# Pre-norm sums from the fourth job's third step to the fifth job's first step, their spread to the third, in a two-block transformer kernel

## What is computed

```python
def rmsnorm(x, g):
    xf = x.astype(jnp.float32)
    y = xf * lax.rsqrt(jnp.mean(xf * xf, axis=-1, keepdims=True) + EPS)
    return (y * g.astype(jnp.float32)).astype(x.dtype)

def swiglu(x, w_gu, w_down):
    gate, up = jnp.split(x @ w_gu, 2, axis=-1)
    return (jax.nn.silu(gate) * up) @ w_down
...
        y = swiglu(rmsnorm(h, ffn1_pre_g[l]), ffn1_w_gu[l], ffn1_w_down[l])
        h = h + 0.5 * rmsnorm(y, ffn1_post_g[l])
        u = rmsnorm(h, mix_pre_g[l])
        proj = u @ w_in[l]
```

## Time and profile before

| | us |
|---|---|
| median of 3 runs (3285.89 to 3286.72) | 3286.0 |
| the profiled execution | 3285.14 |
| its span, first to last instruction | 3283.3 |
| PE busy, of the span | 3253.5 (99%) |
| DVE busy | 2376.6 (72%) |
| ACT busy | 1696.0 (52%) |
| POOL busy | 319.4 (10%) |
| granted TensorE clock, mean | 0.999 |

### The profile page before, as it was taken

The page is one execution under the profiler, slowest core; times in us unless marked ns, Lnnn a source line. Parts: engine busy times, 40 slices in busy tenths (PEclk is TensorE's granted clock), DMA queues, the critical chain, the costliest instruction groups (busy, mean ns, idle before and its releaser), DMA issues.

```text
span 3283.3 us, 51624 instructions
## 1 busy us (share of the span) xinstructions
PE 3253.5 (99%) x20356; PEld 2902.7 (88%) x20356; DVE 2376.6 (72%) x4254; ACT 1696.0 (52%) x3071; POOL 319.4 (10%) x289
## 2 busy tenths in 40 slices
PE   9999999999999999999999999999999999999998
PEld 7999888888899998999888888899988888889998
DVE  7877765766687768776765776697868676658776
ACT  5555553645465545554553654464547374336553
POOL 1000110121010001000200121010000001201000
PEclk9999999999999999999999999999999999999999
DMA  4333433253233332333424253233322222322332
GB/s 142 109 104 123 120 86 87 81 155 91 81 100 105 108 103 89 105 109 110 123 76 119 59 151 103 68 106 105 115 96 92 88 82 69 105 96 96 102 112 84
DMA packets 118562, 332.80 MB, mean 101 GB/s; under 512 B 18984, under 2 KB 21800, under 8 KB 118320
## 3 DMA queue, kind: packets, MB, share of 16 engines
q1 hardware_dynamic: 106352, 308.40, 30.0%
q0 software_dynamic: 11680, 20.56, 3.1%
q10 hardware_dynamic: 288, 0.52, 0.0%
HBM read 306.23 MB, written 4.21 MB: 95 GB/s over the span
## 4 chain that ended last, share of the span: by engine, by line
PE 90%; DVE 7%; ACT 1%; issue 1%; DMA 0%; POOL 0%; DVEq 0%; ACTq 0%
PE PS L827 89%; PE PS L1231 2%; DVE h L2017 1%; DVE acc L1962 1%; DVE tmp L2014 1%; DVE ul L1970 1%; DVE wl L1933 1%; ACT wh L1350 0%; DMA tmp<-tmp 0%; ACT uh L1350 0%; ACT tmp L1350 0%; ACT stk L1350 0%; DVE y_u L2042 0%; DVE lru L2761 0%; DVE stk L2428 0%
## 5 line engine op out<-in xcount | busy, mean ns | idle before, releaser
L1933 DVE TENSOR_TENSOR wl<-raw,wh 128x1024 fp32r<-128x1024 f32 (+2 forms) x633 | 654.3, 1037 | 253.8 <-ACT wh L1350 248.1
L1350 ACT ACTIVATE wh<-raw 128x1024 fp32r<-128x1024 f32 (+2 forms) x637 | 554.1, 875 | 355.2 <-PE PS L827 342.4
L827 PE MATMUL PS<-bh,wh 128*128 128x256 f32 x2520 | 696.3, 276 | 0.0
L827 PE MATMUL PS<-bh,wl 128*128 128x256 f32 x2520 | 696.3, 276 | 0.0
L827 PE MATMUL PS<-bl,wh 128*128 128x256 f32 x2520 | 695.9, 276 | 0.0
L827 PE MATMUL PS<-uh,wh 128*128 128x512 f32 (+2 forms) x1656 | 613.8, 371 | 9.4 <-DVE ul L1970 4.0
L827 PE MATMUL PS<-ul,wh 128*128 128x512 f32 (+2 forms) x1656 | 598.6, 361 | 0.0
L827 PE MATMUL PS<-uh,wl 128*128 128x512 f32 (+2 forms) x1656 | 598.4, 361 | 0.0
L827 PEld LDWEIGHTS PS<-bh,wh 128*128 128x128 f32 x2520 | 473.1, 188 | 0.6
L827 PEld LDWEIGHTS PS<-bh,wl 128*128 128x128 f32 x2520 | 473.0, 188 | 0.6
L827 PEld LDWEIGHTS PS<-bl,wh 128*128 128x128 f32 x2520 | 473.1, 188 | 0.0
(11 more groups left out here) (272 smaller groups left out, 5366.8 us busy)
## 6 DMA issues: line engine op xcount, KB each, us to landing
raw<-in_gu SPq DMA_DIRECT2D x218, 512.0 KB, 3.2
raw<-in_win SPq DMA_DIRECT2D x139, 512.0 KB, 3.4
raw<-in_dn SPq DMA_DIRECT2D x80, 320.0 KB, 3.0
raw<-in_dn SPq DMA_DIRECT2D x40, 512.0 KB, 3.6
raw<-in_wbr SPq DMA_DIRECT2D x72, 256.0 KB, 2.7
raw<-in_wout SPq DMA_DIRECT2D x24, 512.0 KB, 3.2
raw<-in_dn SPq DMA_DIRECT2D x40, 256.0 KB, 2.7
raw<-in_wv SPq DMA_DIRECT2D x20, 512.0 KB, 3.4
```

The source lines that it names most:

```text
L827: return e.matmul(out, lhs, rhs, start=start, stop=stop, skip_group_check=True)
L1350: return e.activation(out, in_, f, scale=scale, **more)
L1933: tt(lo, src, hi, SUB).then_inc(*S.lo.up(("lo", c)))
```

## The change

`begin` runs the fourth job through without a break. The four sum matmuls stand behind the first two steps of the fifth job, and the four spread matmuls behind its sixth step.

```diff
-                n = 0
-                for _ in dense(after, v, "u"):
-                    n += 1
-                    if n == 3:
-                        sums_pre(v)
+                run(after, v)
                 n = 0
                 for _ in dense(more, v, "u"):
                     n += 1
                     if n == 1:
+                        sums_pre(v)
+                    elif n == 3:
                         spread_pre(v)
```

## The result

The changed kernel takes 3308.4 us (median of five runs, 3303.0 to 3308.8) against 3286.0 (five runs as well, 3285.9 to 3288.0): 1.0065 times the time before, 95% interval 1.0054 to 1.0076, so 22.4 us slower by the medians. The forecast was 3297.8, and its range ended at 3304. The sign was right, and the size too small by 10.6 us. The profiled execution is the fastest of the five, 3303.03 us with a span of 3301.2, and so 17.9 us over the profiled span before.

What follows compares the result with a forecast made beforehand. PE, busy 99% of the span, was taken to bound the kernel. Feed-forwards 7.8, mixers 1.5 and stage 6 2.5 us summed to 11.8 us on the profiled 3285.1; with the median 0.9 higher, 3297.8 us, range 3290 to 3304.

Steps and rivals of the forecast that it cites:

- `acc` goes, c4 takes its place: Sums, stages 1 to 6: the wait for `acc` goes, a c4 low-part wait of 0.47 us (stage 2) leaves 0.24 gained.
- `rb` 2.48 us later: Norm: DVE's `rb` comes 2.48 us later in stages 1 to 6, 2.72 in stages 0 and 7.
- The fourth tile: Feed-forwards, fourth tile `g`: PE late by 0.87 us against before, 1.09 in stages 0 and 7.
- The second pair, 1.48 and 1.70: Feed-forwards, second pair's first weight sum: PE late by 1.48 us, 1.70 in stages 0 and 7, fourth tile's delay included.
- The step that failed: Feed-forwards behind the second pair: DVE has more in hand with each pair, so nothing is added.
- Stage 6: Stage 6: PE already waits for late DVE, nothing is in hand, so all of the 2.48 us is paid.
- Mixers: Stages 1 and 4: bank 3 is freed late for the values, PE late by 0.77 us each, 1.5 together.
- the third rival: A further collision per feed-forward, or a late rotation DMA delaying a low part in stages 1 and 4: 17.0 us, 0.13.
- The fourth tile alone (8.8): Feed-forwards: POOL and DVE meet in another order, only the fourth tile holds PE; 8.8 us in all, 0.17.
- More cover: DVE's queue makes up 2 us before the places named, leaving only six gains of 0.24 us: -1.4 us, 0.10.
- The collision's 17.0 us: Contention lengthens DVE's queue by one further collision, 1.05 us, per feed-forward: 17.0 us in all, 0.13.

Runs made afterwards that it cites:

- two of its relatives: The move in the five feed-forward stages alone, 3301.5 us; the sums and spread moved half as far in all stages, 3291.7 us.
- the wide matmul carrying the wait: One more 128x512 matmul per feed-forward stage takes the wait for the second pair's weight sum: changed kernel 3306.4, feed-forwards alone 3298.6, with stage 6 filler 3305.0 us.
- one wide matmul and no wait: The kernel before with one more 128x512 matmul in each of the five feed-forward stages, where it waits for nothing: 3298.9 us.
- rows of 3 to 16: The kernel before with 2, 3, 4, 8 and 16 more 128x512 matmuls in a row in stages 0, 2, 3, 5 and 7: 3300.1 us, one run.
- half the way: Against the kernel before, sums behind the fourth job's eighth step and spread behind the fifth's fourth, in all stages: 3291.7 us.
- the wide matmul in the changed kernel: The changed kernel with one more 128x512 matmul per feed-forward stage, which takes the wait for the second pair's weight sum: 3306.4 us.
- the changed kernel again: The changed kernel measured and profiled a second time, nothing altered: 3309.4 us.

## Why the prediction was wrong in size, step by step

- **`acc` goes, c4 takes its place.** Right: six waits. In stage 2 PE was held for 0.55 us where 0.47 was expected (0.39 shown as idle). The gain kept was 0.1 to 0.3 us by lag, 0.24 expected.
- **`rb` 2.48 us later.** Right, a little short: the spread stands at 909.87 against 903.03, less the 4.23 us lag with which PE came to the place: 2.61.
- **The fourth tile.** Right as a wait: it added 1.1 us in all five stages (0.24 + 0.87 expected in stage 2). Against before PE was 1.0 to 1.1 us late in stages 2, 3 and 5, where 0.87 was expected, and 1.2 in 0 and 7 (1.09).
- **The second pair, 1.48 and 1.70.** Right in sum: of the ten feed-forward stages in the two profiles nine cost 1.53 to 1.80 us in waits as the table counts them, and stage 3 of the first 2.20, where a wait of 0.7 us for `y_u` came on top. What was to be paid at the second pair beyond the tile's 1.1 came half at the first pair (0.24), which had no term, and half at the second (0.24).
- **The step that failed.** "From there on DVE has more in hand with each pair and nothing is added." It was argued from DVE alone. That PE goes on behind a wait at the pace it had was never asked, and the pitch of the 128x256 matmuls, which has two values, has no term. Both values stand in the trace of the kernel before, the slower one ahead of every post-norm, so the possibility could have been read there. 1.8 us are added in each stage that falls in: two of five in both profiles of the changed kernel, four of five in two of its relatives. The last lines of the prediction name it as what would make it wrong ("if PE's time per matmul or the granted clock changes"), with no price. A break in a steady row of matmuls should have been a case of the range.
- **Stage 6.** The size of the wait was right (2.64 and 2.73 against 2.48), its place half so: L2086 was not the first to hold PE but the keys' DMA, then L2067. (The row of DVE behind the earlier trace rows was called gapless; it has one gap of 0.47 us for ACT, which gave nothing back.) What followed, 1.2 to 3.8 us of half clock, was missing.
- **Mixers.** Bank 3 cost 1.17 - 0.20 = 0.97 us against 0.77. In stage 1 another 0.4 to 0.5 us came in the two profiles of the changed kernel (0.04 to 0.75 over all five with the full move there) for a low part behind the late rotation, which is the second half of the third rival. A wait for `stkf` in the later part of stages 1 and 4 moves by -0.7 to +1.4 us, in one case by 3.5, and by 4.2 with the half clock behind it, also in kernels that leave these stages alone; it makes stage 4 cost 0.05 in one profile and 1.79 in the other. It belongs to no term.
- **Rivals.** The fourth tile alone (8.8) is out, as PE is held again at the pairs in all five stages. More cover is out. The collision's 17.0 us comes nearest to the time, by luck: no row shows such a collision, and the excess has other causes.

In sum: 11.8 forecast, 14 measured for the waits, and 5 to 7 us on top in the two profiles, from the slower pitch and the half clock, which were put at nothing. That the medians hold a few us more than the two profiled runs, which were the fastest of their five, fits more stages with the slower pitch. No trace of such a run shows it.

## What to carry to other kernels

Where PE is at its limit, a wait of a quarter microsecond can cost seven times its length on top, since it can change the pitch of hundreds of matmuls behind it. The wait of 1.1 us at the fourth tile, among 128x512 matmuls, cost itself and no more. So a late release is better laid in such a stretch or where something is in hand, and a term for the pitch belongs into the range. Compare two traces by the start of the k-th matmul: it finds losses that neither busy time nor waits show. Look for more than one pitch in the trace before the change, too. If PE must stand still for some microseconds, a few matmuls that nobody reads can be cheaper than the idle time.

## What the runs showed of the hardware

- **Two pitches for one row of instructions.** The 128x256 matmuls of the pairs, each with its own 128x128 weight load, run at 0.1133 or 0.1178 us, granted clock 1.00 in both. Once in, the slower one stayed to the next long row of 128x512 matmuls. Over all profiles, in the five feed-forward stages: with no break in the pairs 0 stages of 25; with an ordinary short wait 15 of 25; with the wide matmul carrying the wait 4 of 15, and in all four it had set in at the first pair, ahead of that matmul; with one wide matmul and no wait 5 of 5; with rows of 3 to 16 4 of 4, with a row of two 0 of 1. The last 78 matmuls ahead of every post-norm have the slower one without any of this, in the kernel before too. The Trainium skill, page "TensorE: Matmul & The Clock Gate", section "Back-to-back issue gap", gives for a matmul by itself one spacing for each number of columns, 262 cycles for 256. At 2.4 GHz that is 0.109 us, an estimate from the page's figure; by these traces there are two, both a little longer. What picks one is open.
- **The clock fell at short idle times of PE, in some places and not in others.** Idle times of about 1.8 and 1.5 us, two matmuls apart, brought 3.4 or 6.8 us at 1.2 GHz, 1.2 to 2.3 us of lag; 0.4 and 1.5 us did so as well in the kernel with half the way. In three of the six profiles (the move in stage 6 alone, the wide matmul in the changed kernel, and the changed kernel again) the clock was down before the second idle time or as it began, in the others near its end or just behind. In four of the six another 3.4 us at half clock came 240 us later, at 2716 to 2733, 1.6 us of lag, behind idle times of 0.56 and 1.45 us that all profiles have. Idle times of 2.0 and 2.1 us elsewhere had the full clock behind them. What decides is open.
- **A gap can hide from the waits.** PE's start 0.27 us behind the last one, rather than 0.11, shows no idle time in the timeline, since the matmul ahead is drawn 0.28 us long.
